# Feed-forward up part: products four and five made of seven smaller ones, six of seven in all

## What is computed

```python
def swiglu(h, w_gate, w_up, w_down):
    return (jax.nn.silu(h @ w_gate) * (h @ w_up)) @ w_down
```

## Time and profile before

| what | value |
| --- | --- |
| time of the runs | 5040.19 us median of 3 (5039.02 to 5042.06) |
| profiled execution | 5038.25 us, its span 5036.5 us |
| TensorE busy | 4925.7 us, 98% |
| VectorE busy | 2962.0 us, 59% |
| ScalarE busy | 861.9 us, 17% |
| L1541, whole products | 480 passes, 209.3 us |
| L1553, split products | 1120 passes, 245.0 us |
| mean granted clock of TensorE | 0.99 |

### The profile page before, as it was taken

How to read it: one execution, slowest core, us unless ns; L and a number is a source line. 1 busy time by engine, 2 the same in 40 slices (tenths; PEclk the granted TensorE clock), 3 DMA queues, 4 the chain that set the end, 5 groups by cost and what they waited for, 6 DMA issues and landing times. The chain is left out here.

```text
span 5036.5 us, 67774 instructions
## 1 busy us (share of the span) xinstructions
PE 4925.7 (98%) x26055; PEld 3404.9 (68%) x26055; DVE 2962.0 (59%) x5158; ACT 861.9 (17%) x1663; POOL 70.4 (1%) x96
## 2 busy tenths in 40 slices
PE   8999999999999999999999799999999999999998
PEld 4545556855466654447666695959788696969695
DVE  3434445645367753453666575757667575767686
ACT  3611211133211100160444100000000000000010
POOL 0000000000000000000000000000000000000110
PEclk9999999999999999999999899999999999999999
DMA  5145032411122263433321354544445454545575
GB/s 209 40 149 181 26 105 96 155 56 62 61 67 71 69 206 100 159 109 117 109 89 55 114 185 149 192 164 160 169 156 189 152 181 176 185 172 201 183 281 217
DMA packets 396600, 694.41 MB, mean 138 GB/s; under 512 B 19896, under 2 KB 171003, under 8 KB 394234
## 3 DMA queue, kind: packets, MB, share of 16 engines
q1 hardware_dynamic: 382072, 641.80, 36.9%
q0 software_dynamic: 9920, 36.19, 2.0%
q10 hardware_dynamic: 4290, 12.11, 0.6%
HBM read 575.21 MB, written 114.83 MB: 137 GB/s over the span
## 5 line engine op out<-in xcount | busy, mean ns | idle before, releaser
L4861 PE MATMUL psum<-arena 128*128 128x128 f32 (+2 forms) x10752 | 1235.7, 276 | 2.6 <-issue 2.2
L4861 PEld LDWEIGHTS psum<-arena 128*128 128x128 f32 x10752 | 1225.8, 191 | 6.6 <-issue 6.6
L4840 PE MATMUL psum<-arena 128*128 128x512 f32 x1568 | 691.0, 596 | 1.8 <-DVE arena L4453 1.8
L4570 DVE TENSOR_TENSOR arena<-arena 128x1024 f32<-128x1024 f32 x448 | 539.4, 1224 | 65.2 <-issue 40.4
L4840 PEld LDWEIGHTS psum<-arena 128*128 128x128 f32 x1568 | 292.6, 190 | 363.2 <-issue 357.9
L1624 PE MATMUL psum<-arena 128*128 128x512 f32 x616 | 265.0, 592 | 0.0
L1553 PE MATMUL psum<-arena 128*128 128x256 f32 x1120 | 245.0, 379 | 0.0
L4745 ACT ACTIVATE arena<-psum 128x288 f32<-128x288 f32 (+1 forms) x112 | 44.6, 398 | 1162.6 <-PE psum L4861 1083.6
L2208 PE MATMUL psum<-arena 128*128 128x256 f32 (+1 forms) x968 | 239.6, 407 | 1.4 <-PEq L112 1.4
L1553 PEld LDWEIGHTS psum<-arena 128*128 128x128 f32 x1120 | 212.8, 190 | 37.5 <-issue 9.6
L4448 DVE TENSOR_TENSOR arena<-arena 128x512 f32<-128x512 f32 x112 | 77.7, 693 | 255.7 <-PE psum L4846 156.7
(11 more groups left out here) (634 smaller groups left out, 6171.1 us busy)
## 6 DMA issues: line engine op xcount, KB each, us to landing
arena<-in_moe_w_gate SPq DMA_DIRECT2D x112, 1024.0 KB, 7.1
arena<-in_moe_w_up SPq DMA_DIRECT2D x112, 1024.0 KB, 7.3
arena<-in_moe_w_down SPq DMA_DIRECT2D x112, 1024.0 KB, 5.2
y_dram<-zeros SPq DMA_DIRECT2D x1, 23040.0 KB
x_dram<-arena SPq DMA_DIRECT2D x32, 512.0 KB, 4.6
arena<-in_ab_w_in SPq DMA_DIRECT2D x7, 2048.0 KB, 9.1
arena<-z_dram SPq DMA_DIRECT2D x8, 1664.0 KB, 7.5
arena<-in_c_w_in SPq DMA_DIRECT2D x6, 2048.0 KB, 11.8
```

Of the source, the lines that this page charges most:

```text
L4570: V.tensor_tensor(to, left, right, ALU.subtract).then_inc(t_up, 1)
L4840: return nc.tensor.matmul(g.ps[:, bank, :], left, right, start=(i == 0), stop=(i == STEPS - 1))
L4861: last = nc.tensor.matmul(g.ps[:, bank, f * HT:f * HT + N // 2], right[:, k, f * P:(f + 1) * P], left[:, k, 0:N // 2], start=(k == 0), sto ...
```

## The change

Products 4 and 5 are made of seven smaller ones as well, so that six of seven are split and only product 1 is whole. SPLIT becomes (2, 3, 4, 5, 6, 7); inner token sums for products 4 and 5 get memory inside `hv` (that of tokens 3 and 2) and are made at the start, those of product 4 with the others and those of product 5 ahead of block 1. Each block gets inner weights 4 and 5 and combinations 4 and 5, and ScalarE's copy of product 4 becomes two corner copies. VectorE's order in a block is written anew, and so are TensorE's waits: product 1 now waits for combination 6 of the block before, product 6 for combination 4, product 7 for combination 5. The three whole-width additions become one. `bring_low(3)` and `bring_low(2)` of the last block move behind products 4 and 5 on SyncE's queue. The store of Q22, which stands behind `load_low(1, 1, 2, b11)` and ahead of `load_low(1, 1, 0, b11)` as before, waits for gate Q22 as before.

```diff
-    SPLIT = (2, 3, 6, 7)
-    inner = [[A.at(o + 512 * q, 2, 256) for q in range(3)] for o in (24576, 26112, 35840, 37376)]
+    SPLIT = (2, 3, 4, 5, 6, 7)
+    WAYS = len(SPLIT)
+    inner = [[A.at(o + 512 * q, 2, 256) for q in range(2)] + [A.at(last, 2, 256)] for o, last in ((24576, 25600), (26112, 27136), (33024, 34560), (30208, 31744), (35840, 36864), (37376, 38400))]
...
-        return 4 * n + SPLIT.index(q) + 1
+        return WAYS * n + SPLIT.index(q) + 1
...
+        def turn(n, q):
+            return WAYS * (n - 1) + SPLIT.index(q)
...
             sp.wait_ge(st_b, 16 * N)
-            bring_low(2)
-            bring_low(3)
             sp.wait_ge(pm, groups_done(N, 3))
...
             for t in (2, 3):
                 fetch_x(t, x_low)
+            bring_low(3)
             sp.wait_ge(pm, groups_done(N, 5))
+            bring_low(2)
             load_low(1, 1, 2, b11)
             store(N, Q22, 1, 1)
             sp.wait_ge(pm, groups_done(N, 6))
...
-                pe.wait_ge(inner_made, it * 8 + (4 * (b - 1) - 3 + at))
+                pe.wait_ge(inner_made, it * (2 * WAYS) + (WAYS * (b - 2) + at + 1))
...
-                    pe.wait_ge(combed, it * 8 + (4 * c - 1))
+                    pe.wait_ge(combed, it * (2 * WAYS) + (WAYS * (c - 1) + 5))
                     whole_product(b, 1)
                     pe.wait_ge(rb2, it * 64 + 32 * c)
                     pe.wait_ge(hidden, 4)
                     pe.wait_ge(x_summed, 1)
-                    pe.wait_ge(combed, it * 8 + 4 * c)
+                    pe.wait_ge(combed, it * (2 * WAYS) + (WAYS * (c - 1) + 6))
                     split_product(it, b, 2)
                     pe.wait_ge(x_summed, 2)
                     pe.wait_ge(outer_made, it * 8 + (4 * c - 2))
-                    pe.wait_ge(whole, it * 4 + (2 * c + 1))
+                    pe.wait_ge(whole, it * 2 + (c + 1))
                     split_product(it, b, 3)
                     pe.wait_ge(outer_made, it * 8 + (4 * c - 3))
-                    pe.wait_ge(combed, it * 8 + (4 * c + 1))
-                    whole_product(b, 4)
+                    pe.wait_ge(combed, it * (2 * WAYS) + (WAYS * c + 1))
+                    pe.wait_ge(x_summed, 3)
+                    split_product(it, b, 4)
+                    pe.wait_ge(x_summed, 6)
+                    pe.wait_ge(outer_made, it * 8 + (4 * c - 1))
+                    pe.wait_ge(combed, it * (2 * WAYS) + (WAYS * c + 2))
+                    split_product(it, b, 5)
+                    pe.wait_ge(rb3, it * 64 + 32 * c)
                     pe.wait_ge(x_summed, 4)
-                    pe.wait_ge(outer_made, it * 8 + (4 * c - 1))
-                    pe.wait_ge(combed, it * 8 + (4 * c + 2))
-                    whole_product(b, 5)
-                    pe.wait_ge(rb3, it * 64 + 32 * c)
-                    pe.wait_ge(x_summed, 3)
-                    pe.wait_ge(whole, it * 4 + (2 * c + 2))
+                    pe.wait_ge(combed, it * (2 * WAYS) + (WAYS * c + 3))
                     split_product(it, b, 6)
                     pe.wait_ge(x_summed, 5)
                     pe.wait_ge(outer_made, it * 8 + 4 * c)
-                    pe.wait_ge(joined, it * 14 + (7 * c + 4))
+                    pe.wait_ge(combed, it * (2 * WAYS) + (WAYS * c + 4))
                     split_product(it, b, 7)
...
-                nc.scalar.activation(corners[SPLIT.index(q) % 2], vector_of(n, q)[:, SLOT[1], :], ACT.Copy).then_inc(corner, 1)
+                nc.scalar.activation(corners[turn(n, q) % 2], vector_of(n, q)[:, SLOT[1], :], ACT.Copy).then_inc(corner, 1)
...
                 take_corner(n, 3)
-                act.wait_ge(st_e, 16 * n)
-                take_whole(n, 4, e5)
+                take_corner(n, 4)
                 if n == N:
                     act.wait_ge(hid, 4 * (N - 1) + Q11)
                     nc.scalar.activation(hv[:, 0:4, K - 1, :], za[:, 0:2, :].rearrange("p a (b t) -> p (a b) t", t=P), ACT.Copy).then_inc(put, 1)
+                take_corner(n, 5)
...
-                y, (w1, w2, w3, w4) = RIGHTS[q - 1], ring[at % 2]
-                own, until = {2: (1, 0), 6: (1, 1)}, {2: groups_done(n - 1, 6), 3: groups_done(n - 1, 7), 6: groups_done(n, 2), 7: groups_done(n, 3)}
-                dve.drain()
-                if n > 1 or q in (6, 7):
-                    dve.wait_ge(pm, until[q])
+                y, (w1, w2, w3, w4) = RIGHTS[q - 1], ring[turn(n, q) % 2]
+                own, two_ago = {2: (1, 0), 6: (1, 1)}, SPLIT[at - 2]
+                dve.drain()
+                if turn(n, q) >= 2:
+                    dve.wait_ge(pm, groups_done(n if at >= 2 else n - 1, two_ago))
...
-                V.tensor_tensor(z[:, 0:4, :] if q != 3 else u, z[:, 0:4, :], add, ALU.add).then_inc(joined, 1)
+                V.tensor_tensor(z[:, 0:4, :] if to is None else to, z[:, 0:4, :], add, ALU.add).then_inc(joined, 1)
...
+            def za_is_free(n):
+                if n < N:
+                    dve.wait_ge(st_a, 16 * 2 * n)
+                else:
+                    dve.wait_ge(put, 1)
             def block_of_features(n):
                 outer(n, t1, raw[0, 1], raw[0, 0])
                 outer(n, t2, raw[1, 1], t1)
                 inner_weights(n, 3)
                 outer(n, t3, raw[1, 1], raw[0, 1])
+                inner_weights(n, 4)
                 dve.wait_ge(st_a, 16 * (2 * n - 1))
-                dve.wait_ge(whole, 2 * n + 1)
+                dve.wait_ge(whole, n + 1)
                 combine(n, 2, za, e1)
+                dve.wait_ge(st_b, 16 * n)
+                combine(n, 3, zb, e1, u)
+                gate(n, Q11)
+                inner_weights(n, 5)
                 outer(n, t4, raw[1, 0], t2)
-                dve.wait_ge(st_b, 16 * n)
-                combine(n, 3, zb, e1)
-                gate(n, Q11)
+                combine(n, 4, zb, u, part)
                 inner_weights(n, 6)
-                dve.wait_ge(whole, 2 * n + 2)
-                V.tensor_tensor(part, u, e5, ALU.add).then_inc(joined, 1)
+                za_is_free(n)
+                combine(n, 5, za, u, u)
+                dve.wait_ge(st_e, 16 * n)
+                dve.drain()
+                V.tensor_tensor(e5, u, zb[:, 0:4, :], ALU.add).then_inc(joined, 1)
                 inner_weights(n, 7)
-                dve.wait_ge(pm, groups_done(n, 5))
-                V.tensor_tensor(u, u, flat_of(n, 5), ALU.add).then_inc(joined, 1)
-                dve.drain()
-                V.tensor_tensor(e5, u, e5, ALU.add).then_inc(joined, 1)
                 if n < N:
                     inner_weights(n + 1, 2)
                 else:
                     sum_tokens(0, ((0, 8), (8, K - 1)))
                 gate(n, Q22)
-                if n < N:
-                    dve.wait_ge(st_a, 16 * 2 * n)
-                else:
-                    dve.wait_ge(put, 1)
                 combine(n, 6, za, part)
...
-            for q in (2, 3, 6):
+            for q in (2, 3, 4, 6):
                 inner_tokens(q)
                 in_place(q).then_inc(x_summed, 1)
             inner_tokens(7)
...
             up(1)
             up(2)
             dve.wait_ge(mm, 4)
-            V.tensor_tensor(s3, a11, a21, ALU.subtract).then_inc(x_summed, 1)
+            V.tensor_tensor(s3, a11, a21, ALU.subtract)
             in_place(7).then_inc(x_summed, 1)
             up(3)
+            inner_tokens(5)
+            in_place(5).then_inc(x_summed, 1)
```

More of the change, by code:

```diff
@@ L1546, in split_product @@
                 at = SPLIT.index(q)
+                slot = (WAYS * b + at) % 2
                 to = all_ps[:, 2048 * ((b + q - 1) % 2):2048 * ((b + q - 1) % 2) + 7 * 256].rearrange("p (a t) -> p a t", t=256)
-                x, y, (i1, i2, i4), (w1, w2, w3, w4) = LEFTS[q - 1], RIGHTS[q - 1], inner[at], ring[at % 2]
+                x, y, (i1, i2, i4), (w1, w2, w3, w4) = LEFTS[q - 1], RIGHTS[q - 1], inner[at], ring[slot]
                 top, low_k = slice(0, 2), slice(2, 4)
@@ L1740, in outer, with combine @@
                 V.tensor_tensor(to, one, two, ALU.subtract).then_inc(outer_made, 1)
-            def combine(n, q, z, add):
-                v, p1 = vector_of(n, q), corners[SPLIT.index(q) % 2]
+            def combine(n, q, z, add, to=None):
+                v, p1 = vector_of(n, q), corners[turn(n, q) % 2]
                 dve.wait_ge(pm, groups_done(n, q))
-                dve.wait_ge(corner, 4 * (n - 1) + SPLIT.index(q) + 1)
+                dve.wait_ge(corner, turn(n, q) + 1)
                 V.tensor_tensor(z[:, 0:5:4, :], v[:, 0:2, :], p1.unsqueeze(1).broadcast_to([P, 2, 256]), ALU.add)
@@ L1879, in take_norm @@
                                 g.mix_g[:, 8:16].unsqueeze(2).broadcast_to([P, KD, P]), ALU.mult).then_inc(n_taken, 1)
-            credit(dve, whole, 2)
-            credit(dve, combed, 4)
+            credit(dve, whole, 1)
+            credit(dve, combed, WAYS)
             credit(dve, joined, 7)
```

## The result

The changed kernel takes 5058.29 us (median of 7 runs, 5054.95 to 5060.44) beside 5039.8 us for the kernel before (7 runs): a ratio of 1.0035, 95% interval 1.0025 to 1.0045. The profiled execution takes 5055.77 us, its span 5053.4 us, against 5038.25 and 5036.5.

What follows compares the result with a forecast made beforehand. TensorE alone set the pace; after the change VectorE's 44.45 us round would stall it. Blocks 2.3, pauses 1.3, end 3.1, clock 1.7 and 1.7 sum to 10.1 us: 5050 predicted, range 5043 to 5066.

Steps and rivals of the forecast that it cites:

- the fall of the clock inside the blocks: In the up part's blocks, one fall of TensorE's clock counted for three blocks with a VectorE pause: 1.7 us.
- TensorE's gain of 1.63 us a block: Products 4 and 5 become split, so TensorE needs 43.14 us a block, 16.3 us less in ten.
- VectorE's queue as the bound: In each up block VectorE needs 44.45 us a round even if it never waits, so TensorE stalls ahead of product 1.
- Where the two meet: Paragraph on the block: product 7 ends 0.4 us late, product 1 stalls 1.5 us for combination 6; 2.3 us in nine blocks.
- The block's length: From one end of product 3 to the next: 45.02 us, 0.25 more than 44.77; VectorE's pauses add 1.3 us in all.
- combination 3 starts at 0.78: In each block VectorE starts combination 3 0.78 us after product 3 ends, with ScalarE's corner copy between.
- The end of the part: After block 10 the last first-down weights load waits behind gate 2's store; down products start 3.1 us later, bounds 0.1 and 5.
- The start of the part: Inner tokens of products 4 and 5, 3.1 us each, are covered by waits: nothing; uncovered they cost 3 us once.
- The clock: 4.3 us of idle ahead of the down products lowers TensorE's clock, 1.7 us; one fall inside the blocks, 1.7 us.
- rival (a): TensorE's clock falls in every up block: 15.3 us in place of the one fall counted, 5064; chance 0.16.
- Rival (d): VectorE keeps up, its round under 43.1 us and combination 6 freeing its half 1.9 us sooner: 5029; chance 0.06.
- The drain rule: On VectorE each instruction waits for an empty pipe: 0.7 us a block, 6.5 in nine; not used in the forecast.

Runs made afterwards that it cites:

- corner experiment: Changed kernel with ScalarE copying the corner of product 3 ahead of the Silu of gate 1: 5053.19 us, 1.0032 to the kernel before.
- gathers moved: Changed kernel with hidden-row loads for tokens 2 and 3 behind both first down weight loads, the last ahead of the store: 1.0026; with VectorE's reordered queue too, 5028.95 us.
- new order alone: Changed kernel with VectorE's instructions reordered (combination 6 right behind the last sum, t1 ahead of gate 4) and corners 3 and 6 ahead of Silus: 0.9989 to the kernel before.
- new order without t1's move: The reordered VectorE and ScalarE queues, but t1 of the next block stays behind gate 4: 5041.2 us in one run, blocks 43.52 us.

## Why the prediction was right, and where it was off

It forecast slower by 10 us (5050, range 5043 to 5066, slower 0.50). Measured: slower by 18.5 us between the medians, 5058.3, inside the range. Between the profiled executions it is 17.5 against 10.1. Of the terms the blocks, the end and the clock behind it came out too small by 5.0, 2.2 and 0.7 us and the scatter outside the part adds 1.2, while the fall of the clock inside the blocks, 1.7 us, never came. That this error ran against the others brought the number closer than its terms were.

- **TensorE's gain of 1.63 us a block:** right. It appears in full (43.13 us) as soon as VectorE lets it.
- **VectorE's queue as the bound:** right in mechanism and place, with one reservation. TensorE waits ahead of product 1 for the fourth instruction of combination 6 (nine times) and in the middle of product 7 for its inner weights (0.64 us; 0.4 foreseen). Combination 6's release comes 25.3 us after the start of combination 3, as summed, and the pauses cost 0.34 us in four of eight blocks, 1.4 us (1.3 foreseen). The reservation: the prediction said that a VectorE idle for over 1 us at a time would refute its sum, and VectorE is idle for 1.07 us ahead of combination 3 in the rows of block 6. Its round of 44.45 us is indeed not the bound. The path is, from T3 through combination 3 to the release by combination 6 and on through products 1 to 3: 1.25 + 25.3 + 0.05 + 6.97 + 12.09 = 45.66. The paragraph "Where the two meet" had this path.
- **The block's length:** mis-sized. 45.02 foreseen, 45.64 measured, 3.6 us in nine intervals against 8.6, pauses included. The first interval, where combination 2 ends before T3, is as foreseen, 45.04. The failed step is "combination 3 starts at 0.78": it took the corner copy's delay from a block in which ScalarE was idle at T3. With weights 4 ahead of it, combination 2 ends at T3 + 0.2 (the prediction's own sums have VectorE through its round 44.45 + 0.78 - 45.02 = 0.21 us behind T3), its Silu goes ahead of the corner, and combination 3 starts at 1.25. The same text said that ScalarE's copies cost nothing since each is over 1 us early; that holds for the added two and not for the old one of product 3. The corner experiment gives exactly this 0.47 us back. A further 0.11 us is in product 1 itself, 6.97 us behind a wait and 6.86 without.
- **The end of the part:** right place, wrong step. 3.1 us more foreseen, 5.3 measured, just outside its bounds of 0.1 and 5. SyncE had issued the gathers by T3 + 19.6 (20 foreseen), and the last load followed gate 2 at T3 + 24.4 (23.8 foreseen, without ScalarE's 0.47). The failed step is "lands 5.1 us later": with the gathers' data still moving it took 6.7. And the wait for the store, to which the prediction gave the whole delay, gives back only 0.5 us while the gathers stand ahead; with the gathers moved too it is 4.5. The cause that it named for its outer bound was there beside the store.
- **The start of the part:** right, at nothing. VectorE's wait of 3.8 us ahead of L1901 (L1913 now) shrank to 0.7, so the inner tokens of product 4 lie within it, and combination 3 of block 1 starts 0.78 us behind T3.
- **The clock:** 1.7 us foreseen at the end, 2.4 measured. The fall inside the blocks (1.7) didn't come, nor did rival (a): over 1425 to 1838 us the granted clock is 1.00 with waits of 0.64 and 1.26 us, some 4 us apart, in each block.
- **Rival (d)**, VectorE keeping up, had its block right (43.1 us), and its condition too: VectorE's round under 43.1 us (42.76 by the intervals) and combination 6 earlier by 1.9 us. The prediction found nothing in the trace that gives it, in the order as written; another order of the same instructions does. Its 5029 us is another matter. With the new order alone it is 5033.5, because the end costs more than the 4.8 us that the rival took off; 5029 is met only with the gathers moved as well, which was no part of the rival.
- **The drain rule** of the Trainium skill ("VectorE: DVE Perf Modes", section "The DRAIN you can't avoid") would have had 0.7 us more a block. The prediction took it without its exception: the same section says that a next instruction that isn't held starts earlier, which is what the 0.35 us between two starts show. The new order without t1's move is bound by VectorE's total, which is 43.54 us by the intervals of the earlier trace rows and was 43.52: the trace's intervals hold.

## What to carry to other kernels

When work moves from a busy engine to one with room, sum the receiving queue from start to start and then follow the path from the resource it frees last; a total below the period isn't enough, as 44.00 and 45.16 us show, and the same instructions in another order gave 43.13. Look also for a third engine's queue that the later end of a step re-orders: a Silu slipped ahead of a copy and cost half a microsecond a block. And a transfer that is moved later meets what was already there; put those needed first ahead of those that are merely possible.

## What the runs showed of the hardware

- How long SyncE takes to issue a gather of hidden rows (640 KB) isn't fixed: four took 5.15 us, the four moved ones right behind them and x 10.19, and two behind the weights, in the kernel with the gathers moved, 1.17. A plain load of weights, 0.38 us before, took 2.46 us behind four gathers. I read a long issue as a sign of transfers still queued; the traces don't show the queue's filling itself.
- Two waits in each block, 0.64 and 1.26 us, leave the granted clock at 1.00 for 413 us, while one of 5.4 us halves it for some 7 us; in the kernel with the new order alone one of 7.2 us does the same. One of 2.54 us, with the gathers moved, left it at 1.00, where in the earlier trace rows 1.84 us of idle went with 0.79: the length of the wait alone doesn't decide it.
- VectorE's pauses of 0.4 us behind nothing visible come at the same instructions in both traces of the changed kernel and in those of its variants with the same VectorE order: blocks 2, 5, 6, 7 and 10, of which the first four lengthen an interval. In the new order there are three, in blocks 6, 8 and 10. What they are stays open; no run here tried it.
